# Sums of squares of a grouped norm split into high and low parts, and two products of 512 columns in place of four in fp32

## The reference

```
y = y + d_skip.astype(jnp.float32)[:, None] * xh.astype(jnp.float32)
y = y.reshape(b, s, SSM_WIDTH) * jax.nn.silu(z.astype(jnp.float32))
y = _rms(y.reshape(b, s, SSM_GROUPS, SSM_WIDTH // SSM_GROUPS)).reshape(b, s, SSM_WIDTH)
return (y * norm_w.astype(jnp.float32)).astype(z.dtype)
```

## Time and profile before

| what | us |
|---|---|
| median of 3 runs | 1158.32 (1156.28 to 1159.64) |
| the profiled execution, its own time | 1160.82 |
| its span, first to last instruction | 1159.1 |
| TensorE busy in it | 1134.6 |
| GpSimd busy | 554.5 |
| VectorE busy | 642.8 |
| ScalarE busy | 525.2 |

### The profile page before, as it was taken

One profiled execution on the slowest core, in us unless ns is written; L12 is line 12 of the kernel. 1 busy time (PEld: TensorE's weight loads), 2 busy tenths in 40 slices (PEclk: granted clock), 3 DMA queues, 4 the chain that ended last, 5 costly groups with the idle time before them and its releaser, 6 DMA issues.

```text
span 1159.1 us, 15472 instructions
## 1 busy us (share of the span) xinstructions
PE 1134.6 (98%) x5986; PEld 936.2 (81%) x5986; DVE 642.8 (55%) x782; ACT 525.2 (45%) x908; POOL 554.5 (48%) x396
## 2 busy tenths in 40 slices
PE   5899999999999999999999999999999999999997
PEld 4678888888888878888898788888888887888886
DVE  5706355569887555437460634565988854132275
ACT  5435256655445533223533535666545553232333
POOL 4534534446445455545804364345545535455551
PEclk7999999999999999999999999999999999999999
DMA  9645423334434445744313462323433523433332
GB/s 321 196 108 176 153 72 85 93 106 127 118 95 107 136 141 163 232 146 121 84 35 92 130 216 74 91 74 109 128 101 99 137 64 90 111 98 103 91 95 88
DMA packets 217225, 139.23 MB, mean 120 GB/s; under 512 B 11928, under 2 KB 207552, under 8 KB 217152
## 3 DMA queue, kind: packets, MB, share of 16 engines
q1 hardware_dynamic: 216504, 137.59, 41.2%
q10 hardware_dynamic: 648, 0.66, 0.2%
HBM read 135.08 MB, written 2.62 MB: 119 GB/s over the span
## 4 chain that ended last, share of the span: by engine, by line
PE 92%; POOL 3%; DVE 2%; DMA 1%; ACT 1%; SPq 0%; issue 0%; DVEq 0%
PE main L618 79%; PE psC L618 4%; PE psB L618 4%; PE psA L618 4%; POOL w_lo L544 3%; DMA zs<-in_w_ada 1%; PE psB L826 1%; PE psB L806 1%; DVE psC L1375 1%; DVE h_lo L1412 0%; ACT w_hi L1018 0%; SPq L364 0%; DVE tmp L1407 0%; ACT h_hi L1018 0%; PE psC L835 0%
## 5 line engine op out<-in xcount | busy, mean ns | idle before, releaser
L544 POOL TENSOR_TENSOR w_lo<-raw,w_hi 128x512 fp32r<-128x512 f32 x344 | 507.8, 1496 | 557.9 <-ACT w_hi L1018 557.6
L618 PE MATMUL main<-h_hi,w_hi 128*128 128x512 f32 (+1 forms) x1104 | 439.2, 398 | 7.3 <-DVE h_lo L1412 6.3
L618 PE MATMUL main<-h_hi,w_lo 128*128 128x512 f32 (+1 forms) x1104 | 428.6, 388 | 0.0
L618 PE MATMUL main<-h_lo,w_hi 128*128 128x512 f32 (+1 forms) x1104 | 428.1, 388 | 0.0
L1018 ACT ACTIVATE w_hi<-raw 128x512 fp32r<-128x512 f32 x344 | 199.5, 623 | 304.3 <-PE main L618 219.9
L618 PEld LDWEIGHTS main<-h_hi,w_hi 128*128 128x128 f32 x1104 | 208.4, 189 | 61.5 <-issue 15.8
L618 PEld LDWEIGHTS main<-h_hi,w_lo 128*128 128x128 f32 x1104 | 208.3, 189 | 43.4
L618 PEld LDWEIGHTS main<-h_lo,w_hi 128*128 128x128 f32 x1104 | 208.7, 189 | 41.5 <-issue 1.9
L1683 DVE TENSOR_TENSOR tmp<-main,misc 128x512 f32<-128x512 f32 x32 | 22.1, 691 | 172.0 <-PE main L618 168.4
L1529 DVE SCALAR_TENSOR_TENSOR misc<-main,cols,misc 128x511 f32<-128x511 f32 (+2 forms) x96 | 71.9, 749 | 65.2 <-ACT misc L1018 62.5
L618 PE MATMUL main<-y_hi,w_hi 128*128 128x512 f32 x256 | 100.5, 393 | 0.0
(11 more groups left out here) (248 smaller groups left out, 1255.7 us busy)
## 6 DMA issues: line engine op xcount, KB each, us to landing
raw<-in_w_in SPq DMA_DIRECT2D x124, 512.0 KB, 3.8
xbc<-in_w_ada SPq DMA_DIRECT2D x16, 512.0 KB, 4.9
zs<-in_w_ada SPq DMA_DIRECT2D x16, 512.0 KB, 4.4
raw<-in_w_pc SPq DMA_DIRECT2D x16, 512.0 KB, 4.0
raw<-in_w_out SPq DMA_DIRECT2D x16, 512.0 KB, 4.0
zs<-in_w_ada SPq DMA_DIRECT2D x16, 256.0 KB, 7.2
xbc<-in_w_in SPq DMA_DIRECT2D x8, 512.0 KB, 7.4
big<-in_w_ada SPq DMA_DIRECT2D x16, 256.0 KB, 7.2
```

The source lines that it names most:

```text
L544: nc.gpsimd.tensor_tensor(lo_b[:, cut, :], raw_b[:, cut, :], hi_b[:, cut, :].bitcast(F32), ALU.subtract).then_inc(s_split[b], 2 * BT_ // kt)
L618: return nc.tensor.matmul(o, a, b_, start=start, stop=stop)
```

## The change

In pairs 0, 1 and 2 of each layer, six times in all, the paired squares are no longer multiplied in fp32. ScalarE rounds them to fp32r (into slot p+5 of `y_hi`, which is free at that time), GpSimd subtracts to get the low part (slot p+5 of `y_lo`), and TensorE makes two products of 512 columns, all four groups at once, with a column of ones in fp32r. Pair 3 is as before.

```diff
+        ones_r = sb("ones_r", [P, 1], F32R)
...
+        s_sqh2, s_sql2, s_onesr = sem("y_squares_hi"), sem("y_squares_split"), sem("ones_r_done")
...
             pool.sem_inc(s_const, 1)
+            nc.gpsimd.tensor_copy(ones_r[:, :], ones[:, :]).then_inc(s_onesr, 1)
...
                     nc.gpsimd.tensor_tensor(sq[:, :, 0], sq[:, :, 0], sq[:, :, 1], ALU.add).then_inc(s_ysum, 1)
+                    if p < PAIRS - 1:
+                        pool.wait_ge(s_sqh2, l * (PAIRS - 1) + p + 1)
+                        hi, lo = (t[:, BT_ + p + 1, :].rearrange("p (g n) -> p g n", n=PAIR) for t in (y_hi, y_lo))
+                        nc.gpsimd.tensor_tensor(lo, sq[:, :, 0], hi.bitcast(F32), ALU.subtract).then_inc(s_sql2, 1)
...
             def norm_mm(l, p):
+                if p < PAIRS - 1:
+                    pe.wait_ge(s_onesr, 1)
+                    pe.wait_ge(s_sql2, l * (PAIRS - 1) + p + 1)
+                    one = ones_r[:, 0:1].broadcast_to([P, P])
+                    mm(psC1, one, y_hi[:, BT_ + p + 1, :], True, False)
+                    mm(psC1, one, y_lo[:, BT_ + p + 1, :], False, True).then_inc(s_yn, 1)
+                    return
                 pe.wait_ge(s_ysum, l * PAIRS + p + 1)
...
                     f(at(y_hi, p + BT_), buf_b, ACT.Copy).then_inc(s_ybh, 1)
+                    if p < PAIRS - 1:
+                        act.wait_ge(s_ysum, l * PAIRS + p + 1)
+                        f(y_hi[:, BT_ + p + 1, :].rearrange("p (g n) -> p g n", n=PAIR),
+                          buf_x.rearrange("p (g t n) -> p g t n", t=2, n=PAIR)[:, :, 0], ACT.Copy).then_inc(s_sqh2, 1)
                     sigmoid(1)
```

## The result

| | before | changed |
|---|---|---|
| median us (runs) | 1158.88 (4) | 1186.76 (4) |
| lowest to highest | 1156.28 to 1159.64 | 1185.07 to 1187.80 |
| profiled execution: time, span | 1160.82, 1159.1 | 1186.40, 1184.6 |
| mean granted clock | 0.988 | 0.979 |

The ratio is 1.0248, 95% interval 1.0235 to 1.0261: slower by 27.9 us. The forecast was 1181, with a range from 1172 to 1186. The way was right, but the time lies 0.8 us above the range: the loss was 4.9 us larger than worked out.

The account below looks back on a forecast made before the run. TensorE, busy for 1134.6 of 1159.1 us, was taken to bound the kernel. Stall 16.6 plus clock falls 6.4 made +23.0 on the median 1158.3: 1181 us, range 1172 to 1186.

Parts of the forecast that it names:

- The bound and the chain at the place: TensorE bounds all; at six places GpSimd's subtraction and split halves alternate with VectorE's scans, TensorE waiting for the split.
- the list of what would show it: Trace signs: subtraction 3.0 to 3.1 us, halves 3.3 and 1.3, TensorE idle about 0.4 and 2.5, clock 0.50 behind most places.
- The stall, 6 x 2.76 = 16.6: At six places TensorE reaches the transposes 2.76 us later, waiting for the delayed weight split; 16.6 us in all.
- The turns at the port, against sharing: VectorE and GpSimd alternate whole instructions at their port; rival: they share it, +3.9 us, 1162.2, chance 0.04.
- The rival in which the subtraction gets in first: Subtraction beats the first scan, then turns: TensorE 1.4 us later per place, +8.4, 1166.7; chance 0.05.
- the rival on the other side (-4.3): GpSimd does subtraction and both halves in a row before the scan: 0.72 us gained per place, 1154.0; chance 0.03.
- four falls of six, 6.4 us: TensorE's granted clock falls to 0.50 behind four of the six stalls, about 1.6 us each; rival without falls 1174.9, chance 0.25.
- the upper bound of 9.6: Most the clock was taken to cost: a fall at each of the six places, 9.6 us.
- The gain of the products: Norm products on TensorE take 0.46 us, not 0.81: 0.35 per place, 2.1 in six, vanishing in the next tile's wait.
- the new wait (b): TensorE's next tile waits for its split's first half, starting at 282.62, where its 13th product starts before the change.
- the old wait at the 13th product: Before the change, TensorE loses about 0.3 us in the next tile, waiting for GpSimd's second split half; the change removes it.
- Cover: Existing waits hide ScalarE's copy, the cast of the ones column and VectorE's later steps, so these cost nothing.

Follow-up runs that it names:

- fill: Changed kernel plus ten 512-column products, into PSUM nobody reads, behind the norm products of pairs 0 to 2; 1174.15 us, ratio 1.0143 to before.
- subdve: Changed kernel with the subtraction moved from GpSimd to VectorE, ahead of the two scans; 1154.33 us, ratio 0.9971 to before.
- hold: Changed kernel with one more wait: VectorE starts its two scans only when GpSimd's subtraction is done; 1153.01 us, ratio 0.9955 to before.
- nosub: Changed kernel without GpSimd's subtraction; both products take the high part, ScalarE's copy and TensorE's wait for it stay; 1158.30 us, ratio 0.9999 to before.
- before_hold: Kernel before, fp32 norm products kept, with VectorE's scans waiting for the first half of the next weight split; 1154.64 us, ratio 0.9968 to before.
- subonly: Changed kernel's copy and subtraction, but TensorE keeps the four fp32 products, which wait only for the pairing; 1185.29 us, ratio 1.0239 to before.
- the last three kernels here: Scans waiting for the subtraction, 1153.01 us; subtraction on VectorE with scans waiting for the first split half, 1152.29; kernel before with that latter wait, 1154.64.

## Why the prediction was wrong

**The bound and the chain at the place: right.** TensorE bounds the kernel, and the place behaves as worked out from the four timelines. Subtraction: expected 279.33 - 276.25 = 3.1, measured 3.10. First half 3.24, second 1.27, for 3.3 and 1.3. The tile waits 2.51, for 2.5. The norm products are idle for 0.63 to 0.78, for the 0.4 in the list of what would show it, and start 0.8 to 0.9 late by the steps, for the 0.7 in the text: a small miss, which vanishes in the tile's wait as worked out.

**The stall, 6 x 2.76 = 16.6: right.** `fill` isolates it: 16.7 from pairing to pairing, 16.3 by the medians.

**The turns at the port, against sharing: right.** `subdve` and `hold` show it in both directions. The rival in which the subtraction gets in first and the scan, queued already, goes next (+8.4 us) wasn't seen in that form. `hold` is near it: the subtraction goes first, but VectorE begins its scan only afterwards, at 274.85, when GpSimd has begun the first half at 274.78, so that two of GpSimd's instructions go in a row; it is *faster* than before, by 3.2 us at the six places. That has the sign of the rival on the other side (-4.3), but isn't its order: the second half comes behind the scan and takes 3.28.

**The clock, "four falls of six, 6.4 us": wrong, and this is the step that failed.** It measured 11.8 us. The mechanism, a fall of the clock behind the stall, was right; its size was off in two ways. The clock fell at six places of six. And its price isn't one number: four falls took about 3.4 us and cost 1.5 to 1.6 each, near the 1.6 assumed, but two, behind the second pairs, lasted 6.7 us and cost 2.7 and 2.9. Not even the upper bound of 9.6 held it, as it took each fall for as long as the one in the earlier trace rows. The other two falls between the start and the end of that execution, at 142 and 702, were equally long, so reading them too wouldn't have shown the longer kind; only the start of the program has a longer stretch, 0.50 from 15.8 to 29.2 us. I had let a fall cost less if it begins while TensorE still waits. The two that did so most clearly, about 1.0 and 0.7 us before the tile's first product (320.98 and 894.11), are the two long and dear ones. And I had tied the fall to an emptier stretch ahead of it: the one at 142 came behind 3.30 us in which the profile shows TensorE busy throughout. The sum with what was measured, 16.7 + 11.8 = 28.5, is within 0.6 of the 27.9 of the medians.

**The gain of the products: right that it vanishes**, but for one reason too few. I let it vanish in the new wait (b). `nosub` shows that it would have vanished without the change's stall as well, in the old wait at the 13th product. That wait was also worth more than I read: I put it at 0.27 and the restart at 0.1, and `before_hold`, which is without it, gained 0.4 to 0.6 at a place. I repeated the mistake in what I expected of `nosub`, though the earlier trace rows had all that was needed: the 13th product can't start before GpSimd's half is done, however early the products before it are.

**Cover: right.** ScalarE's copy and the cast cost nothing that shows (`nosub`), nor do VectorE's later steps (the stall in `fill` is 2.75 to 2.80 at each place, for 2.76).

## What to carry to other kernels

An instruction added to an engine that is half idle isn't paid by its own length but by its turn: read what the other engine on the port does at that moment, and who gets in first. Before a cheaper step is counted as a gain, find the next wait behind it and ask who ends that wait; if it isn't the step, the gain is nil, and here one line that ordered two engines (`before_hold`, 3.3 us) was worth more than the cheaper products at their best (2.6). And when TensorE is made to stand still, the clock can be a cost beside the stall, here 1.5 to 2.9 us at a place beside 2.8 of stall. Read its price from all the falls a trace has, and still count a longer one among the bounds.

## What was not expected of the hardware

- A difference of 0.13 us in who begins, scan or split half, changes the half from 3.27 to 1.30 us (`subdve`, first and second pair). The one trace has both orders, the same one at the same pair of either layer.
- The granted clock stayed at 0.50 for 6.7 us behind the second pairs, although TensorE waited there no longer than elsewhere (2.51 us). `subonly` has the same pattern, two long falls behind the second pairs and four short ones. In both kernels a long fall begins 0.7 to 1.0 us before the tile's first product, a short one between 0.2 us before it and 0.5 behind. What made these falls twice as long was not tried.
- Ten useless products of 512 columns at each place made the changed kernel faster by some 12 us, which is what its falls of the clock had cost.
- Falls of the clock at places that no edit touched (at 53.5 us before, not in the changed kernel's trace) are worth about 1.5 us each, which is of the size of the differences between the medians of the last three kernels here (0.7 to 2.4 us).
